# Value products over cached pages: page outermost with four requests inside, and one mark for all four

## The chip, the cores and the metric

The kernel runs on one core of a Trainium2 chip. The metric is device time in microseconds (us) of one execution; the time of the kernel before is the median of three runs. TensorE (PE) multiplies, VectorE (DVE), ScalarE (ACT) and GpSimd (POOL) do the rest, and SyncE (SP) issues most of the loads. The engines run on their own and meet at semaphores.

## The reference, cut to what matters

The program is one step of a two-layer decoder. Each layer serves one prompt of 1024 tokens and 8 sample requests of 4 tokens. Its mixer has three head groups (forgetting attention "FoX", RWKV-7, retention), then an output projection and a gated feed-forward. The change lies in FoX attention of the sample requests. Each request has 8 cached pages of 128 keys and of 128 values, with 8 heads of 64, found through a page table:

```python
def fox_sample(q, k, v, logf, k_past, v_past, logf_past):
    ...
    s_past = jnp.einsum('bthd,bshd->bhts', q, k_past, preferred_element_type=F32) * scale
    s_past = s_past + (cn[..., :, None] - cp[..., None, :])
    ...
    p = jax.nn.softmax(jnp.concatenate([s_past, s_new], -1), axis=-1).astype(v.dtype)
    return (jnp.einsum('bhts,bshd->bthd', p[..., :P], v_past)
            + jnp.einsum('bhts,bshd->bthd', p[..., P:], v))
```

The change concerns the product of the weights `p[..., :P]` with the cached values `v_past`. All is float32.

## The kernel before

Everything is written per engine, with the order by hand: a block for SP, POOL, PE, DVE and ACT, each a list of instructions with waits on semaphores. No scheduler moves anything. `Steps` numbers the marks that an engine sets in one pass of a loop (`G_PE`: PE's marks in a pass over one group of requests), so that others can wait for "mark V2 of pass it". A mark rides on the last matmul of a step.

The 8 requests are served in two groups of four: in each layer a loop `g` runs twice, `it = 2*l + g`, four passes in all. One group puts its four requests side by side in 128 partitions: request b owns partitions 32b to 32b+31 (`NS` is 32: 4 tokens by 8 heads). In one pass PE does:

- `bias`: the forget terms go to PSUM banks 0 to 2.
- For each request b, the key pages are transposed (`key_tr`, marks `T{b}{p}`, line 764 of the helper `tr`), ACT or DVE copies them out, and the scores are added to PSUM (`S{b}{p}`, helper `mm`, line 760). `p` counts pairs of heads.
- DVE and ACT do the softmax over all four requests. PE transposes the weights (`P0`, `P1`, `Pn`) into `pts`, which lies in the tile that the profile calls `hT`.
- The value products, which this change touches: first one product with the new tokens' values (`pnt` by `vn`), which opens all 128 partitions of PSUM bank 7. Then, for request b, wait for its pages, and for its eight pages j multiply `pts[:, j, 32b:32b+32]` (128 keys by 32 columns) by `slot[b][:, j, :]` (128 keys by 512) into partitions 32b to 32b+31 of bank 7. The last one carries mark `V{b}`. In the profile these are the rows `ps<-big,hT 128*32 128x512`: `slot` lies in the tile `big`. One call of `mm` in float32 gives two MATMUL instructions, each with its own weight load (engine PEld).
- DVE masks bank 7 into `om` (line 1885), PE gathers the heads (`F`, `ps<-wd 128*128 128x16`), and DVE writes the output (line 1888).

`slot[b]` holds eight pages of request b: first keys, then, when these are transposed (`T{b}3`), its values. SP loads keys (line 512) and the first five value pages (line 519), POOL the other three (line 737). On SP's queue a pass is: for b in 0 to 3, wait for `V{b}` of the pass before (line 508, the slot is free), eight key loads; then, for b in 0 to 3, wait for `T{b}3`, five value loads. Each load is preceded by a read of the page number. After the second pass of a layer SP waits for `F` and loads the weights `w_out`.

`norm_sum` (line 772) is used below as a comparison. It sends three products `ps<-sil,ones 128*32 128x352` to partitions 0, 32 and 64 of one PSUM bank, one after another.

Of the kernel before, what the change touches and what calls it, by code (L numbers as in the profile page):

```python
# [24 lines left out]
NPG, PG = 8, 128  # L25
# [13 lines left out]
NS = DB * TS  # L39
# [75 lines left out]
def build(nc, I, O, decay_rows):  # L115

    ctx = ExitStack()
    with ctx:
# [229 lines left out]
        fgr_dve, fgr_act, fgr_pe = (sem(f"foxgroup_{x}") for x in ("dve", "act", "pe"))  # L348
# [25 lines left out]
        def job_psum_tm(j):  # L374
# [66 lines left out]
                      "sn", "mx", "mn", "max", "neg", "sum", "rec", "pn", "pne", "pt1", "pnt", "om", "o")  # L441
        G_ACT = Steps(*[f"kt{b}{p}" for b in range(4) for p in (0, 2)], "e", "en", "pt0")
        G_PE = Steps("bias", *[x for b in range(4) for x in [f"T{b}0"] + [y for p in range(4) for y in ([f"T{b}{p + 1}"] if p < 3 else []) + [f"S{b}{p}"]]],
                     "P0", "P1", "Pn", "V0", "V1", "V2", "V3", "F", first=5)

        block = ctx.enter_context(nc.Block())
        w_in = I["w_in"]
# [3 lines left out]
        def _(sp):  # L451
# [31 lines left out]
            with sp.Fori(0, DEPTH) as l:  # L483
                for j in range(RING, 8):
                    free(l, j)
                    load(l, j, w_block(l, w_in, RFC[j]))
                for j0, c0_, n in ((J_EQ, C_EQ, 4), (J_EV, C_EV, 4), (J_FQ, C_FQ, 8), (J_FV, C_FV, 4)):
                    for j in range(j0, j0 + n):
                        free(l, j)
                        load(l, j, w_block(l, w_in, c0_ + P * (j - j0)))  # L490

                sp.wait_ge(table_in, 16)
                sp.wait_ge(fg_dve, FG_DVE.at(l, "vn"))
                sp.wait_ge(fp_pool, FP_POOL.at(l * 4 + 3, "k"))
                sp.wait_ge(fox_out, l * 16 + 16)
                sp.wait_ge(fox_out2, l * 16 + 16)
                sp.sem_inc(passed, 1)
                with sp.Fori(0, 2) as g:
                    it = l * 2 + g
                    for b in range(4):  # L500
                        if b == 3:

                            sp.wait_ge(fp_act, FP_ACT.at(l * 2 + 1, "1oT"))
                            sp.wait_ge(lft_out, l * 32 + 32)
                            sp.wait_ge(ko_out, l * 128 + 128)
                            sp.sem_inc(passed, 1)

                        sp.wait_ge(fgr_pe, G_PE.at(it - 1, f"V{b}"))
                        sp.sem_inc(passed, 1)
                        for j in range(NPG):  # L510
                            page = sp.value_load(ptab[0:1, bass.ds(g * (4 * NPG) + (b * NPG + j), 1)], min_val=0, max_val=N_POOL - 1)
                            sp.dma_start(slot[b][:, j, :], I["cache_fox_k"][bass.ds(l, 1), bass.ds(page, 1)].rearrange("a n p h d -> p (a n h d)")).then_inc(page_in[b], 16)

                    for b in range(4):
                        sp.wait_ge(fgr_pe, G_PE.at(it, f"T{b}3"))
                        sp.sem_inc(passed, 1)
                        for j in range(V_SP):
                            page = sp.value_load(ptab[0:1, bass.ds(g * (4 * NPG) + (b * NPG + j), 1)], min_val=0, max_val=N_POOL - 1)
                            sp.dma_start(slot[b][:, j, :], I["cache_fox_v"][bass.ds(l, 1), bass.ds(page, 1)].rearrange("a n p h d -> p (a n h d)")).then_inc(page_in[b], 16)
                    sp.sem_inc(passed, 1)  # L520

                sp.wait_ge(fgr_pe, G_PE.at(l * 2 + 1, "F"))
                for j in range(J_OUT, J_OUT + RING):
                    sp.sem_inc(passed, 1)
                    free(l, j)
                    load(l, j, w_block(l, I["w_out"], P * (j - J_OUT)))
                for j in range(J_OUT + RING, J_FF):
                    free(l, j)
                    load(l, j, w_block(l, I["w_out"], P * (j - J_OUT)))

                with sp.Fori(0, FT // 2) as q:
                    for u in range(RING):
                        sp.wait_ge(gemm_done, l * PJOBS + q * RING + (J_FF + u - RING + 1))
                        load(l, u, w_block(l, I["w_gate" if u % 2 == 0 else "w_up"], q * (2 * P) + P * (u // 2)))

                for j in range(2):
                    if j == 0:
                        sp.wait_ge(gemm_done, l * PJOBS + J_OUT + 1)
                    sp.dma_start(wd[:, j, :, :], w_block(l, I["w_down"], P * j)).then_inc(down_loaded[j], 16)
                for j in range(2, KT):  # L540
                    sp.wait_ge(gemm_done, l * PJOBS + J_DOWN + j - 2 + 1)
                    sp.dma_start(wd[:, j % 2, :, :], w_block(l, I["w_down"], P * j)).then_inc(down_loaded[j % 2], 16)

                for j in range(RING):
                    sp.wait_ge(gemm_done, l * PJOBS + JOBS - RING + j + 1)
                    sp.sem_inc(passed, 1)
                    load(0, j, w_block(DEPTH - 1 - l, w_in, RFC[j]))
# [210 lines left out]
        def _(pe):  # L758
# [53 lines left out]
            with pe.Fori(0, NTT // 2) as t:  # L812
                for u in range(2):
                    pe.wait_ge(x_in[u], t * 16 + 16)
                    pe.wait_ge(xt_ev, t * 2 + u + 1)
                    for k in range(KT):
                        last = tr(ps[:, 4 * u + k // 4, P * (k % 4):P * (k % 4) + P], xstage[:, u, P * k:P * k + P])
# [3 lines left out]
            for k in range(KT):  # L821
                last = tr(ps[:, 0, NS * k:NS * k + NS], xstage[0:NS, 0, P * k:P * k + P])
# [4 lines left out]
            with pe.Fori(0, DEPTH) as l:  # L827
# [7 lines left out]
                for m in range(2):  # L835
                    for s, (name, r0) in enumerate((("w", 0), ("a", 32))):
# [9 lines left out]
                        for b, (a, e) in enumerate(((0, 512), (512, 1024), (1024, XW))):  # L846
                            last = mm(ps[:, 4 * s + b, 0:e - a], lora[r0:r0 + 32, P * m:P * m + P], xs[r0:r0 + 32, 6, a:e])
                        PR_PE.mark(last, pr_pe, f"{name}{m}")
                for m in range(2):
                    pe.wait_ge(pr_dve, PR_DVE.at(l, f"ksq{m}"))  # L850
                    pe.wait_ge(pr_act, PR_ACT.at(l, "a1"))
                    for b, (a, e) in enumerate(((0, 512), (512, 1024), (1024, XW))):
                        last = mm(ps[:, 4 * m + b, 0:e - a], blk[:, :], sq1[m][:, a:e])
# [32 lines left out]
                with pe.Fori(0, NTT) as c:  # L886
                    it = l * NTT + c
# [58 lines left out]
                    last = mm(ps[:, 7, 0:RW], sg[64:P, :], lora[64:P, :])  # L946
# [6 lines left out]
                    for h in range(RH):  # L953
                        last = tr(ps[:, 0, P * h:P * h + P], sl[8][:, h, :])
# [13 lines left out]
                    last = x_values(3)  # L968
# [7 lines left out]
                    for h in range(RH):  # L976
                        last = mm(ps[:, 2, HD * h:HD * h + HD], sl[8][:, pos(h), :], x0(h))
# [5 lines left out]
                    for h in range(RH):  # L983
                        last = mm(y_out_(h), sl[2][:, pos(h), :], uu(h), False, True)
                    RW_PE.mark(last, rw_pe, "Y")
                    for h in range(RH):
                        last = mm(s_out(h), btok(h), uu(h), False, True)
# [6 lines left out]
                    for m in range(2):  # L994
                        last = tr(ps[:, 6, P * m:P * m + P], sl[6][:, m, :])
# [4 lines left out]
                for m in range(2):  # L1000
                    last = tr(ps[0:HD, 0, P * m:P * m + P], st[:, m, :])
# [10 lines left out]
                for m in range(2):  # L1012
                    for b in range(DB):
                        last = tr(ps[:, m, HD * b:HD * b + HD], nat[0:HD, b, P * m:P * m + P])
# [3 lines left out]
                for h in range(RH):  # L1018
# [4 lines left out]
                    last = mm(ps[SR, 4 + h % 2, NS * m:NS * m + NS], ars[r, m, 0, :], bts[r, m, :])  # L1023
                RS_PE.mark(last, rs_pe, "L")
                for m in range(2):
# [3 lines left out]
                    last = mm(ps[SR, 7, 256 + 2 * m:258 + 2 * m], rk2s[:, m, :], col2("rk", 2 * m))  # L1029
# [3 lines left out]
                for h in range(RH):  # L1033
                    last = mm(ps[SR, 0, NS * h:NS * h + NS], smat[1][SR, h, :], smat[0][SR, h, :])
# [3 lines left out]
                for h in range(RH):  # L1038
                    last = mm(ps[SR, 1, NS * h:NS * h + NS], smat[2][SR, h, :], smat[3][SR, h, :])
                RS_PE.mark(last, rs_pe, "Z2")  # L1040
                last = mm(ps[SR, 7, 0:RW], sgs[64:P, :], lora[64:P, :])
# [3 lines left out]
                for h in range(RH):  # L1045
                    m, r = h // 2, half(h)
                    o = ps[SR, 2 + h % 2, HD * m:HD * m + HD]
                    for b in range(DB):
                        mm(o, aex[r, m, b, :], sts[r, m, b, :], b == 0, False)
                    last = mm(o, smat[5][SR, pos(h), :], vts(h), False, True)  # L1050
# [3 lines left out]
                for h in range(RH):  # L1054
                    last = mm(ps[SR, 6, HD * h:HD * h + HD], smat[3][SR, pos(h), :], hd(x0s, h))
# [3 lines left out]
                for h in range(RH):  # L1059
                    m, r = h // 2, half(h)  # L1060
                    o = ps[SR, 4 - h % 2, HD * m:HD * m + HD]
# [3 lines left out]
                    last = mm(o, smat[4][SR, pos(h), :], hd(us, h), False, True)  # L1065
                RS_PE.mark(last, rs_pe, "Y")
                pe.wait_ge(*dv("vex3"))
                for h in range(RH):
                    m, r = h // 2, half(h)
                    o = ps[r, m, :]  # L1070
                    mm(o, vbks[SR, 2 + m, half(h)], uex[SR, h].rearrange("p b d -> p (b d)"), True, False)
                    last = mm(o, vbks[SR, 4 + m, half(h)], vex[SR, h].rearrange("p b d -> p (b d)"), False, True)
# [3 lines left out]
                for m in range(2):  # L1076
                    last = tr(ps[:, 6, NS * m:NS * m + NS], yns[SR, P * m:P * m + P])
# [40 lines left out]
                with pe.Fori(0, NTT) as c:  # L1118
                    it = l * NTT + c
# [136 lines left out]
                with pe.Fori(0, 2) as g:  # L1256
# [45 lines left out]
                    for b in range(4):  # L1302
                        pe.wait_ge(page_in[b], it * ((NPG + V_SP) * 16) + (NPG + V_SP) * 16)
                        pe.wait_ge(vpage_in[b], it * ((NPG - V_SP) * 16) + (NPG - V_SP) * 16)
                        o = slice(NS * b, NS * b + NS)
                        for j in range(NPG):
                            last = mm(ps[o, 7, :], pts[:, j, o], slot[b][:, j, :], False, j == NPG - 1)
                        G_PE.mark(last, fgr_pe, f"V{b}")

                    pe.wait_ge(*gd("om"))  # L1310
                    for p in range(4):
# [49 lines left out]
        def _(v):  # L1361
            def on(*waits):
                for s, val in waits:
                    v.wait_ge(s, val)
# [55 lines left out]
            with v.Fori(0, DEPTH) as l:  # L1420
# [423 lines left out]
                with v.Fori(0, 2) as g:  # L1844
# [36 lines left out]
                    gm(v.tensor_copy(pts[:, 4:8, :], ps[:, 4, :].rearrange("p (j r) -> p j r", j=4)), "pt1")  # L1881
                    on(gp("Pn"))
                    gm(v.tensor_copy(pnt[SR], ps[SR, 5, 0:P]), "pnt")
                    on(gp("V3"))
                    gm(v.tensor_tensor(om.rearrange("p (h d) -> p h d", h=FH), ps[:, 7, :].rearrange("p (h d) -> p h d", h=FH),
                                       shead.unsqueeze(2).to_broadcast((P, FH, HD)), ALU.mult), "om")
                    on(gp("F"))
# [389 lines left out]
```

## Time and profile before

| | us |
|---|---|
| median of 3 runs | 5240.82 |
| lowest and highest | 5238.62, 5245.79 |
| span of the profiled execution, first to last instruction | 5223.1 |
| PE busy in the span | 4683.3 (90%) |
| chain that ended last, PE's share | 82% |
| value products, four bursts together | 99.1 |

The profile has no total of its own for the profiled execution, only its span; the median is 17.7 us above the span. Reading: a timeline row gives the start, the time from the first start to the last end, the engine, line and operation, `out<-in` by tiles, the stationary shape (128*32 is 128 rows by 32 columns) and the moving one, and the count; in brackets the idle time of that engine just before, and what ended it. The matmuls' ends are modelled, their starts are recorded. PEclk is the granted TensorE clock: 1.00 is 2.4 GHz, 0.50 is 1.2 GHz.

### The profile page before, as it was taken

Reading aid. Unit: us, or ns where it says so; the run is one execution under the profiler, and the core shown is the slowest. Engines: PE = TensorE matmul, PEld = TensorE weight load, DVE = VectorE, ACT = ScalarE, POOL = GpSimd, SP = SyncE. Lnnn points to the kernel's source line nnn. Section 1 sums busy time; section 2 is a strip of 40 time slices with the busy share of each in tenths; the row PEclk is TensorE's granted clock in tenths of the full one; section 3 lists DMA queues with packets and bytes.
Section 4 is the critical chain, followed back from the end, with each engine's and each line's share of the span. In section 5 each row is a group of like instructions: output and inputs, shape, how many; then the busy total and the mean of one; then the engine's idle time right before and its main releaser. Section 6 shows DMA issues by size and latency. Waiting matters only on the chain.

```text
span 5223.1 us, 55407 instructions
## 1 busy us (share of the span) xinstructions
PE 4683.3 (90%) x20862; PEld 3164.5 (61%) x20862; DVE 1092.1 (21%) x2491; ACT 654.3 (13%) x1105; POOL 260.1 (5%) x456
## 2 busy tenths in 40 slices
PE   7688888988889999999995879898888999999998
PEld 4477576755445666666654766666653456666665
DVE  2344222133212000000024541312332110000001
ACT  0222011133100000000003220102231000000000
POOL 1000002100000000000010000130000000000000
PEclk8888787989899999999997888798998999999999
DMA  3300101102241111111112001011024211112011
GB/s 75 17 0 0 38 21 23 42 26 65 93 139 33 36 40 36 36 41 34 39 38 5 0 5 41 13 35 42 13 65 157 86 33 36 36 36 58 22 34 61
DMA packets 274079, 215.20 MB, mean 41 GB/s; under 512 B 23696, under 2 KB 236912, under 8 KB 272640
## 3 DMA queue, kind: packets, MB, share of 16 engines
q1 hardware_dynamic: 255296, 163.64, 12.2%
q0 software_dynamic: 18624, 49.50, 3.4%
q8 instruction: 93, 1.52, 0.1%
q14 instruction: 66, 0.54, 0.1%
HBM read 197.55 MB, written 15.53 MB: 41 GB/s over the span
## 4 chain that ended last, share of the span: by engine, by line
PE 82%; DVE 7%; issue 5%; ACT 3%; DMA 3%; DVEq 0%; POOL 0%; ACTq 0%; POOLq 0%; SPq 0%
PE ps L760 79%; PE ps L764 3%; DMA out_rwkv_shift_sample<-big 1%; DVE hT L1379 1%; ACT wd L2136 1%; DMA big<-in_x_prompt 0%; DVE big L1571 0%; DMA wd<-in_state_rwkv 0%; ACT wd L2123 0%; ACT big L2106 0%; DMA out_y_prompt<-big 0%; ACT sil L2152 0%; DVE sil L1372 0%; DVE big L1579 0%; DVE big L1541 0%
## 5 line engine op out<-in xcount | busy, mean ns | idle before, releaser
L760 PE MATMUL ps<-hT,ring 128*128 128x352 f32 x6528 | 1966.1, 463 | 25.6 <-DVE hT L1379 10.7
L760 PEld LDWEIGHTS ps<-hT,ring 128*128 128x128 f32 x6528 | 1246.7, 192 | 738.7 <-issue 29.1
L760 PE MATMUL ps<-big,wd 128*128 128x352 f32 (+3 forms) x2576 | 711.6, 439 | 65.5 <-ACT big L1969 42.3
L760 PEld LDWEIGHTS ps<-big,wd 128*128 128x128 f32 (+2 forms) x2576 | 462.5, 192 | 311.5 <-ACT big L1969 42.6
L1901 DVE TENSOR_TENSOR big<-ps,sil 128x1056 f32 x44 | 55.3, 1258 | 1189.5 <-PE ps L760 1189.5
L760 PE MATMUL ps<-wd 128*128 128x128 f32 (+4 forms) x1560 | 235.0, 297 | 70.0 <-ACT wd L2136 21.7
L760 PE MATMUL ps<-big 128*128 128x128 f32 (+4 forms) x1488 | 244.0, 337 | 52.5 <-POOL big L636 14.8
L760 PEld LDWEIGHTS ps<-wd 128*128 128x128 f32 (+2 forms) x1560 | 207.1, 203 | 136.5 <-issue 76.2
L760 PE MATMUL ps<-ring,hT 128*128 128x128 f32 (+1 forms) x2304 | 261.5, 275 | 0.0
L764 PE MATMUL ps<-ident,big 128*128 128x128 f32 (+4 forms) x998 | 175.4, 322 | 95.4 <-ACT big L1992 28.3
L760 PEld LDWEIGHTS ps<-ring,hT 128*128 128x128 f32 (+1 forms) x2304 | 256.9, 183 | 5.2 <-issue 2.4
L760 PEld LDWEIGHTS ps<-big 128*128 128x128 f32 (+2 forms) x1488 | 203.5, 222 | 86.1 <-issue 16.7
L764 PEld LDWEIGHTS ps<-ident,big 128*128 128x128 f32 (+4 forms) x998 | 131.3, 162 | 123.3 <-issue 67.5
L2164 ACT ACTIVATE sil<-ps 128x1056 f32<-128x1056 f32 x44 | 46.3, 1051 | 1162.8 <-PE ps L760 1162.8
L760 PE MATMUL ps<-sil,wd 128*128 128x64 f32 (+2 forms) x544 | 175.4, 438 | 3.6 <-ACT sil L2152 3.6
L1906 DVE TENSOR_TENSOR xT<-ps,xT 128x1056 f32<-128x1056 f32 x16 | 20.1, 1257 | 599.9 <-PE ps L760 599.9
L2123 ACT ACTIVATE wd<-wd,big 128x256 f32<-128x256 f32 (+7 forms) x128 | 99.2, 775 | 301.7 <-DVE big L1805 301.7
L764 PE MATMUL ps<-ident,wd 128*128 128x128 f32 (+1 forms) x644 | 104.2, 298 | 35.7 <-DVE wd L1877 18.1
L760 PE MATMUL ps<-big,sil 64*128 64x64 f32 (+4 forms) x560 | 116.9, 391 | 8.3 <-DVE sil L1710 8.3
L760 PE MATMUL ps<-ring,wd 128*128 128x128 f32 (+1 forms) x584 | 90.2, 300 | 36.5 <-ACT wd L2136 25.7
L760 PE MATMUL ps<-big,ring 128*128 128x352 f32 x384 | 121.4, 459 | 0.0
L760 PE MATMUL ps<-sil 64*128 64x256 f32 (+4 forms) x608 | 81.8, 420 | 40.6 <-DVE sil L1489 37.7
(336 smaller groups left out, 3122.6 us busy)
## 6 DMA issues: line engine op xcount, KB each, us to landing
big<-in_cache_fox_k SPq DMA_DIRECT2D x128, 256.0 KB, 2.9
ring<-in_w_in SPq DMA_DIRECT2D x60, 512.0 KB, 3.8
ring<-in_w_gate SPq DMA_DIRECT2D x44, 512.0 KB, 3.8
ring<-in_w_up SPq DMA_DIRECT2D x44, 512.0 KB, 3.8
wd<-in_w_down SPq DMA_DIRECT2D x16, 1408.0 KB, 7.0
big<-in_cache_fox_v SPq DMA_DIRECT2D x80, 256.0 KB, 4.0
big<-in_cache_fox_v POOLq DMA_DIRECT2D x48, 256.0 KB, 4.3
ring<-in_w_out SPq DMA_DIRECT2D x16, 512.0 KB, 4.1
```

Of the source, the lines that this page charges most:

```text
L760: return pe.matmul(out, lhsT, rhs, start=start, stop=stop, skip_group_check=True)
L764: return pe.transpose(out, in_, ident[0:n, 0:n])
L1379: NRM_DVE.mark(v.scalar_tensor_tensor(hT[:, k, :].rearrange("p (a b) -> p a b", a=3), xT[:, k, :].rearrange("p (a b) -> p a b", a=3), col( ...
L1901: v.tensor_tensor(big[:, bass.ds((q * 2 + u) * NT, NT)].rearrange("p (a b) -> p a b", a=3), job_psum(1), sil[:, u * NT:(u + 1) * NT].rearr ...
L1906: v.tensor_tensor(xk, job_psum(j), xk, ALU.add).then_inc(evac[j % 2], 1)
L2123: fm(act(sp_[:, s % 2, 0:w], sp_[:, s % 2, 0:w], ACT.Exp, bias=nmx[:, s:s + 1], accum_out=rsum[:, s:s + 1]), f"{u}e{s}")
L2136: fm(a.copy(ptt[:, 0, 0:s // 2 + 1, :], ps[:, 4:6, :].rearrange("p a (b c) -> p (a b) c", c=P)[:, 0:s // 2 + 1, :]), f"{u}pt{s}")
L2164: act(sil[:, u * NT:(u + 1) * NT].rearrange("p (a b) -> p a b", a=3), job_psum(0), ACT.Silu).then_inc(evac[0], 1)
```

## The change

The loop over requests first waits for the pages of all four. Then the loop over pages is outside and the loop over requests inside. Four marks `V0` to `V3` become one mark `V`; SP waits for it before the key loads of every request, and DVE before `om`. The number and the shapes of the products are as before.

```diff
                     for b in range(4):
                         pe.wait_ge(page_in[b], it * ((NPG + V_SP) * 16) + (NPG + V_SP) * 16)
                         pe.wait_ge(vpage_in[b], it * ((NPG - V_SP) * 16) + (NPG - V_SP) * 16)
-                        o = slice(NS * b, NS * b + NS)
-                        for j in range(NPG):
+                    for j in range(NPG):
+                        for b in range(4):
+                            o = slice(NS * b, NS * b + NS)
                             last = mm(ps[o, 7, :], pts[:, j, o], slot[b][:, j, :], False, j == NPG - 1)
-                        G_PE.mark(last, fgr_pe, f"V{b}")
+                    G_PE.mark(last, fgr_pe, "V")
...
-                        sp.wait_ge(fgr_pe, G_PE.at(it - 1, f"V{b}"))
+                        sp.wait_ge(fgr_pe, G_PE.at(it - 1, "V"))
...
-                    on(gp("V3"))
+                    on(gp("V"))
```

On PE, at the value products of a pass. `ps` is PSUM, `pages_in{b}` and `last_v_pages_in{b}` are the semaphores of the loads by SP and by POOL. Before:

```order
L760 MATMUL ps<-ring,wd 128x512 [waits foxgroup_act]
L1303 REGISTER_ALU
L1304 ISA [waits pages_in0]
L760 MATMUL ps<-big,hT 32x512 [waits last_v_pages_in0]
L760 MATMUL ps<-big,hT 32x512 x7
L760 MATMUL ps<-big,hT 32x512 [waits last_v_pages_in1,pages_in1]
L760 MATMUL ps<-big,hT 32x512 x7
L760 MATMUL ps<-big,hT 32x512 [waits last_v_pages_in2,pages_in2]
L760 MATMUL ps<-big,hT 32x512 x7
L760 MATMUL ps<-big,hT 32x512 [waits last_v_pages_in3,pages_in3]
L760 MATMUL ps<-big,hT 32x512 x7
```

The same place now:

```order
L760 MATMUL ps<-ring,wd 128x512 [waits foxgroup_act]
L1303 REGISTER_ALU
L1304 ISA [waits pages_in0]
L760 MATMUL ps<-big,hT 32x512 [waits last_v_pages_in2,pages_in2,pages_in3,last_v_pages_in1,last_v_pages_in3,pages_in1,last_v_pages_in0]
L760 MATMUL ps<-big,hT 32x512 x31
```

The waits for requests 1 to 3 have moved ahead of the first product, and the 32 products stand in one row with no wait between them; which request each belongs to, these rows don't show (the diff does).

On SP, where the key loads of request 1 begin (`ptab` is the page table, `foxgroup_pe` the semaphore of PE's marks); difference of the two:

```order
 L512 DMA big<-in_cache_fox_k 128x512
-L508 REGISTER_ALU
 L511 ISA [waits foxgroup_pe]
 L511 TENSOR_LOAD ptab
```

The wait stays ahead of each request's loads; the register that held the number of `V{b}` is no longer stepped, since all four wait for the same mark.

## Rows read from the trace of the kernel before

**Rows 1.** Page, part 4: shares of the chain that ended last.
```profile
PE 82%; DVE 7%; issue 5%; ACT 3%; DMA 3%; DVEq 0%; POOL 0%; ACTq 0%; POOLq 0%; SPq 0%
```
**Rows 2.** Groups by line and shape, whole span: busy us, mean ns, idle before.
```profile
L760 PE MATMUL ps<-big,hT 128*32 128x512 f32 x256 | 99.1, 631 | 0.0
```
**Rows 3.** Timeline, layer 1: first value burst, and the second pass's keys.
```profile
1417.90 25.01 PE L760 MATMUL ps<-big,hT 128*32 128x512 f32 x64
1428.38 40.81 SPq L512 DMA_DIRECT2D big<-in_cache_fox_k  x32
...
1449.58 3.67 PE L764 MATMUL ps<-ident,big 128*128 128x128 f32 x16
...
1474.49 1.97 PE L764 MATMUL ps<-ident,big 128*128 128x128 f32 x16
```
**Rows 4.** Timeline, layer 1: second value burst to the output projection.
```profile
1470.17 30.10 SPq L519 DMA_DIRECT2D big<-in_cache_fox_v  x20
...
1507.52 24.58 PE L760 MATMUL ps<-big,hT 128*32 128x512 f32 x64
...
1538.54 4.47 PE L760 MATMUL ps<-hT,ring 128*128 128x352 f32 x8 [4.59 <-DMA ring<-in_w_out]
...
1547.57 2.53 PE L760 MATMUL ps<-big,ring 128*128 128x352 f32 x8
1549.94 2.53 PE L760 MATMUL ps<-hT,ring 128*128 128x352 f32 x8
```
**Rows 5.** Timeline of PE, layer 2: both value bursts.
```profile
3991.64 24.97 PE L760 MATMUL ps<-big,hT 128*32 128x512 f32 x64
...
4081.22 24.55 PE L760 MATMUL ps<-big,hT 128*32 128x512 f32 x64
```
**Rows 6.** Timeline of PEld: weight loads early in the first burst, then request 0 to 1.
```profile
1418.76 0.18 PEld L760 LDWEIGHTS ps<-big,hT 128*32 128x32 f32 x1 [0.68 <-issue]
1419.61 0.18 PEld L760 LDWEIGHTS ps<-big,hT 128*32 128x32 f32 x1 [0.68 <-issue]
...
1425.07 0.11 PEld L760 LDWEIGHTS ps<-big,hT 128*32 128x32 f32 x1 [0.32 <-issue]
1425.49 0.14 PEld L760 LDWEIGHTS ps<-big,hT 128*32 128x32 f32 x3 [0.32 <-issue]
1425.92 0.14 PEld L760 LDWEIGHTS ps<-big,hT 128*32 128x32 f32 x2 [0.29 <-issue]
1426.35 0.14 PEld L760 LDWEIGHTS ps<-big,hT 128*32 128x32 f32 x2 [0.29 <-issue]
```
**Rows 7.** Timeline, one norm_sum: six products to three column groups, and what follows.
```profile
1568.96 0.15 PEld L760 LDWEIGHTS ps<-sil,ones 128*32 128x32 f32 x6 [0.49 <-issue]
1568.97 0.79 PE L760 MATMUL ps<-sil,ones 128*32 128x352 f32 x6
...
1569.69 0.86 PE L760 MATMUL ps<-hT,ring 128*128 128x352 f32 x2
```
**Rows 8.** Windows, layer 1: PE, PEld, DVE, ACT, POOL busy, PEclk, DMA share, GB/s.
```profile
1412.56:1422.80 10.24, 9.07 (x17) 3.26 (x18) 1.35 (x4) 1.87 (x2) 0.00 (x0) 0.50 0.13 49
...
1446.69:1453.52 6.83, 6.83 (x23) 4.77 (x22) 0.23 (x1) 1.01 (x1) 0.00 (x0) 0.50 0.74 212
1501.31:1511.55 10.24, 8.21 (x16) 3.09 (x17) 2.14 (x6) 0.59 (x1) 0.00 (x0) 0.50 0.16 59
...
1535.44:1542.27 6.83, 3.73 (x7) 2.22 (x8) 0.00 (x0) 0.00 (x0) 0.00 (x0) 0.50 0.99 282
```
**Rows 9.** Request 0's key loads, second pass (timeline), and landings, 1425 to 1445.
```profile
1428.38 9.56 SPq L512 DMA_DIRECT2D big<-in_cache_fox_k  x8
...
big<-in_cache_fox_k SPq DMA_DIRECT2D x13, 256.0 KB, 2.9
```
**Rows 10.** Request 3's value loads, first pass (timeline), and landings, 1455 to 1505.
```profile
1405.60 5.05 SPq L519 DMA_DIRECT2D big<-in_cache_fox_v  x5
...
big<-in_cache_fox_v SPq DMA_DIRECT2D x20, 256.0 KB, 3.9
```

More of the change, by code:

```diff
@@ L443, in build @@
         G_PE = Steps("bias", *[x for b in range(4) for x in [f"T{b}0"] + [y for p in range(4) for y in ([f"T{b}{p + 1}"] if p < 3 else []) + [f"S{b}{p}"]]],
-                     "P0", "P1", "Pn", "V0", "V1", "V2", "V3", "F", first=5)
+                     "P0", "P1", "Pn", "V", "F", first=5)
         block = ctx.enter_context(nc.Block())
```

## Prediction

> **What bounds the kernel now.** The chain that ended last comes first: PE holds 82% of it [rows 1], so time taken from PE on that chain counts in full until something else is late. Next the groups by shape: the value products are 256 MATMUL instructions, 99.1 us of PE [rows 2]. That is the whole stage the change touches, and no other engine works for PE in it. The timeline shows it as four bursts of 64 instructions, one per pass, of 25.0, 24.6, 25.0 and 24.6 us [rows 3 to 5]. Nobody has work beside a burst except SP, which loads the next pass's keys during the first burst of a layer [rows 3].
>
> The question is how densely the 64 stand. The weight loads tell. Within a request one follows the other at 0.85 us at the low clock and 0.43 us at the high one [rows 6]; all 16 instructions of a request go to the same 32 columns of the array. At the passage from request 0 to 1 the picture differs: three loads within 0.14 us, then twice two [rows 6]. The tail of request 0 and the head of request 1 run side by side, since they use different columns. Without that, a first burst would be 4.9 us at the low clock (1417.9 to 1422.8, [rows 3, 8]; 5.8 instructions of 0.85) and 58.2 of 0.43, 30.0 us with 0.2 for the last one's end. It takes 25.0, so each of the three passages saves 1.7 us, four instructions. The overlap across columns exists already, but only at three points of a burst.
>
> **The change part by part.**
>
> *The order of the products.* With pages outside, two instructions of request 0 are followed by two each of requests 1, 2 and 3, in four different column groups. Whether they then run four abreast is the main term. Norm_sum has this form for three groups: six weight loads start within 0.15 us, and the next stage's first matmul starts 0.72 us after the first of the six [rows 7]. One after the other, at the spacing of the same 352-column form (eight in 2.37 us, 0.30 each, [rows 4]), they would need 1.78; two steps abreast need 0.60 and one end. So three groups, three different moving operands and one PSUM bank don't brake each other. At a passage between requests, request 1 starts while three of request 0's instructions still stand in front [rows 6]; to start request 3 abreast in a page, one each of requests 0, 1 and 2 must be passed, also three. I take four abreast: 16 steps for 64 instructions.
>
> A burst then takes: first pass, 4.9 us at the low clock (5.8 steps), 10.2 steps of 0.43, 0.2 for the end: 9.5 us. Second pass: low from 1507.5 to 1511.55 [rows 4, 8], 4.7 steps, then 11.3 of 0.43: 9.1 us. I let the clock rise as long after the burst's start as now, because what precedes the burst on PE is unchanged. The ends: at the high clock throughout 7.1 us, at the low one throughout 13.8. I take the middle, where the rows lie. Saved: 15.5 us per burst, of which not all is kept.
>
> The Trainium skill, "TensorE: Matmul & The Clock Gate", Part 3 (Packing small matmuls), gives 2.38-fold for three column groups of 32 with 512 moving columns. The share of the ideal carried over to four groups would be 3.17-fold, an estimate: 11.2 us for a first burst in place of 9.5, and about 5201 us in all. The trace's norm_sum gives 1.78 over 0.72, 2.5-fold, but a train of 16 steps pays its end once and one of two steps pays it at a half; so the rows' sum stands.
>
> *The mark and SP's key loads.* Now SP may load request 0's next keys once V0 is done. The last load of V0 stands at 1426.35, its matmul one step later, with some 0.6 us to run [rows 2, 6]: done at 1427.4, and the first key load is issued 1.0 us later, at 1428.38. Eight issues take 9.56 us, the last starts at about 1437.6 and lands 2.9 us later, at 1440.5 [rows 9]. PE takes those keys at 1449.58 [rows 3], so 9.1 us of slack hide them. With the change the mark comes at the end of the burst, 1417.9 + 9.5 = 1427.4, by chance when V0 came. The keys are thus there at 1440.5 as now, 13.1 us after the burst's end, but PE is ready 6.7 us after it (1442.9 to 1449.58 now). This becomes a new wait of 6.4 us in the first pass of each layer: PE's key transposes start at 1440.5, not at 1434.1. The gain there is 15.5 - 6.4 = 9.1 us.
>
> Queued behind SP's wait are the 32 key loads and the 20 value loads of the second pass. Their spacing is SP's own: 40.81 us for 32 [rows 3], 10.2 per request. PE took 24.9 us from request 0's keys to request 2's (1449.58 to 1474.49, [rows 3]), the first of the two the slower, since it began at the low clock [rows 8]. SP needs 20.4 for two, so request 2's keys would be there at 1460.9 and asked for at 1465.4, and request 1's lie between with some 2 us of cover. No second wait.
>
> *The joint wait for values.* In the first pass the last of request 3's SP loads is issued by 1410.7 and landed by about 1414.2 [rows 10], before the burst at 1417.9. So the joint wait ends before the burst; it costs nothing, 3.7 us of cover. In the second pass PE comes 9.1 us earlier while SP's key loads don't, so the cover shrinks: value loads begin at 1470.17 as now [rows 4], four sets at some 6.0 us (5.05 and the next set's wait and first page number), the last issued at 1493.2 and landed at 1497.1. The burst would start at about 1498.4. Cover 1.3 us; I price the wait at 0, at most 2 us.
>
> *The end of a layer.* After the second burst nothing is prefetched that the burst hides: `w_out` is issued after F in both orders, and its 4.6 us wait [rows 4] stays. The second burst's 15.5 us are kept.
>
> *The clock after it.* PE now idles before the key transposes, and the work that lifts the clock is cut in two. Now the clock is back 3.9 us after 1449.58 and 3.7 us after 1538.54 [rows 3, 4, 8]; the longest stretch at the low level here, 1412.56 to 1422.80, is 10.2 us [rows 8]. If it comes back later by 0 to 6 us, half of that is lost: 0 to 3 us after each burst. Nearest are the two values at 3.7 to 3.9, so I take small losses, 1.0 us at the keys, 0.5 at `w_out`.
>
> Sum per layer: 9.1 - 1.0 + 15.5 - 0.5 = 23.1; two layers 46.2. The trace's span would go from 5223.1 to 5176.9, and with the 17.7 us between span and median the median from 5240.8 to 5194.6 us.
>
> **The rivals.**
>
> *Fewer abreast.* If only three groups run at once, a burst has 21.3 steps, 11.8 and 11.4 us; gains 6.8 and 13.2, less 1.5, 18.5 per layer: 5203.8 us. If two, 32 steps, 16.4 and 16.0 us: 2.2 + 8.6 - 1.5 = 9.3 per layer, 5222.2. For it speaks that no row shows four groups at once; against it that three run without a brake and that neighbours overlap at all three passages, by the sum of 30.0 against 25.0 us above.
>
> *No overlap, slower.* If each request's pair must be done before the next request's may start, the page order takes away the three overlaps that exist and adds the key wait: a burst of 30.0 us (29.6), 5.0 more each, and 6.4 of key wait in the first pass, with 1.5 of clock: 17.9 per layer, 35.8 in all, 5276.6 us. The sign turns where bursts last 20.9 us (25.0 + 24.6 less 6.4 and 1.5, halved), 42 steps: fewer than 1.5 products abreast in the mean. The six loads in 0.15 us speak against it. The same page of the Trainium skill, Part 3, says that a weight load overlaps with running matmuls only if the row groups differ; here all use the same 128 rows, and by that rule this rival would hold. The trace disagrees: three loads within 0.14 us over the same rows while request 0 was still running [rows 6].
>
> *The waits eat it.* The gain stays on paper if keys or values land later than worked out, for instance because value loads of POOL now meet SP's key loads sooner. Only the first pass's 9.1 us and some of the second's can go: at worst 2 x 9.1 lost, 5213 us.
>
> **How the numbers follow.** Four abreast 82%, with waits as worked out or up to that worst case; three abreast 4%; two abreast 6%; none 6%; and 2% that the two effects cancel. The forecast is 5194.6. With every burst at the high clock: 11.5 + 17.5 per layer without clock loss, 58 us, 5182.8. With every burst at the low clock and clock losses of 2.9 and 1.6: 4.8 + 10.8 - 4.5 = 11.1 per layer, 5218.6. Allowing 2 us for the spread of medians, the range is 5181 to 5221; the pairs and the no-overlap case lie outside. A measurement of this kernel tells 0.2%, some 10 us, from no change: faster 0.92, same 0.02, slower 0.06.
>
> **What would show it.** Right: bursts of 8 to 11 us with weight loads in clusters of about eight per 0.85 us; a new idle time of PE before the keys' transposes put down to a key load, 4 to 8 us, in the second pass of each layer only; the `w_out` wait as now. Wrong: loads still one per 0.43 us (no overlap), or in threes or twos (fewer abreast); PE idle before the first value product, put down to a value load; a stretch at clock 0.50 that covers whole bursts. The forecast fails most simply if the fourth column group or SP's key loads don't behave as their nearest rows do.

## The result, and the profile after

The changed kernel took 5190.91 us in the median of four runs (5186.18 to 5192.62), the kernel before 5241.09 (5238.62 to 5245.79): ratio 0.9911, 95% interval 0.9891 to 0.9932. It is faster, by 50 us against the 46 forecast, and 3.7 us from the forecast time.

The groups by shape over the whole span, to set against [rows 2]:

```profile
L760 PE MATMUL ps<-big,hT 128*32 128x512 f32 x256 | 38.0, 760 | 0.0
```

The same 256 instructions occupy PE for 38.0 us instead of 99.1. The mean of one has grown from 631 to 760 ns: no single instruction became faster (its modelled length is 1.06 us at the low clock and 0.59 at the high one in both traces); four run side by side, and a larger share of them at the low clock. The timeline of layer 1, to set against [rows 3, 4, 6]:

```profile
1424.39 0.20 PEld L760 LDWEIGHTS ps<-big,hT 128*32 128x32 f32 x8 [1.50 <-issue]
1424.39 9.43 PE L760 MATMUL ps<-big,hT 128*32 128x512 f32 x64
1425.25 0.20 PEld L760 LDWEIGHTS ps<-big,hT 128*32 128x32 f32 x4 [0.66 <-issue]
...
1429.36 0.12 PEld L760 LDWEIGHTS ps<-big,hT 128*32 128x32 f32 x4 [0.50 <-issue]
1429.79 0.12 PEld L760 LDWEIGHTS ps<-big,hT 128*32 128x32 f32 x4 [0.31 <-issue]
...
1434.88 9.56 SPq L512 DMA_DIRECT2D big<-in_cache_fox_k  x8
...
1437.11 4.00 PE L760 MATMUL ps<-wd 64*128 64x512 f32 x6 [1.39 <-DVE wd L1856]
1447.10 3.68 PE L764 MATMUL ps<-ident,big 128*128 128x128 f32 x16 [6.00 <-DMA big<-in_cache_fox_k]
...
1473.03 1.97 PE L764 MATMUL ps<-ident,big 128*128 128x128 f32 x16
...
1476.44 23.52 SPq L519 DMA_DIRECT2D big<-in_cache_fox_v  x20
...
1506.06 9.56 PE L760 MATMUL ps<-big,hT 128*32 128x512 f32 x64
1522.18 5.06 PE L760 MATMUL ps<-hT,ring 128*128 128x352 f32 x8 [4.67 <-DMA ring<-in_w_out]
...
1534.71 2.53 PE L760 MATMUL ps<-hT,ring 128*128 128x352 f32 x8
```

The first row holds the loads of two steps. After it four weight loads lie within 0.12 us at the high clock (0.20 at the low one), and the next four follow one step later: 0.85 us at the low clock, 0.43 at the high one. A burst is 16 steps. The row of key loads has request 0's eight alone, to set against the 9.56 us of [rows 9]. Behind the first burst stands the new wait, 6.00 us, put down to a key load. No burst has a wait for value pages ahead of it, and the wait for `w_out` is 4.67 us (4.6 before). Layer 2:

```profile
3977.57 9.43 PE L760 MATMUL ps<-big,hT 128*32 128x512 f32 x64
...
4000.17 3.68 PE L764 MATMUL ps<-ident,big 128*128 128x128 f32 x16 [5.90 <-DMA big<-in_cache_fox_k]
4059.18 9.58 PE L760 MATMUL ps<-big,hT 128*32 128x512 f32 x64
```

The windows, to set against [rows 8]; the figure behind the five busy times is the granted clock:

```profile
1418.96:1429.20 10.24, 8.98 (x35) 3.38 (x39) 1.44 (x4) 1.87 (x2) 0.00 (x0) 0.50 0.15 58
...
1436.02:1453.09 17.07, 9.99 (x25) 5.65 (x26) 2.04 (x6) 1.01 (x1) 0.00 (x0) 0.50 0.72 201
1500.88:1511.12 10.24, 9.23 (x35) 3.38 (x39) 1.19 (x4) 0.58 (x1) 0.00 (x0) 0.50 0.16 61
1517.94:1528.18 10.24, 6.00 (x10) 3.53 (x11) 0.00 (x0) 0.00 (x0) 0.00 (x0) 0.50 0.77 205
```

The clock is low for 4.8 us of the first burst and 5.1 of the second, then for 6.0 us from the start of the key transposes (3.9 before) and 6.0 from the start of `w_out` (3.7 before).

**Where the time went.** From the first burst's start to the second's, layer 1 took 89.6 us [rows 3, 4] and takes 81.7: 7.9 saved. From the second burst's start to the fifth group of `w_out`, the row at 1549.94 in [rows 4] and at 1534.71 after, it took 42.4 and takes 28.7: 13.8 saved. That is 21.7 us, and layer 2 saves as much.

For all kernels below, one stretch is measured from the starts in the trace: from the last score product of a layer's first pass to the hundredth 128x352 product of `w_out`, both layers added. "Rest" is the span less the stretch.

| kernel | stretch, us | rest, us |
|---|---|---|
| before, first profile | 325.1 | 4898.0 |
| before, second profile (e0) | 322.8 | 4906.1 |
| changed | 281.6 | 4906.3 |
| changed again (e7) | 281.5 | 4909.9 |
| e1, old order, one wait, one mark | 336.6 | 4896.4 |
| e2, pairs | 296.4 | 4906.0 |
| e3, own marks | 278.5 | 4895.1 |
| e4, page numbers ahead | 274.5 | 4906.2 |
| e5, fill | 262.2 | 4907.6 |
| e6, fill and page numbers | 253.7 | 4917.1 |
| e8, more fill | 253.9 | 4899.7 |
| e9, as e6 | 258.8 | 4919.9 |
| e10, as e5 | 265.5 | 4907.4 |

The change is worth 42 us in the stretch (324.0 less 281.5). The rest holds the same instructions in every kernel here, but that SP reads request 0's page numbers earlier in e4, e6, e8 and e9; it spreads over 25 us between profiles. The medians' 50 us, 40 when the changed kernel was run again (e7), and the 35 between the two profiles' spans are those 42 with this spread.

### The profile page after: what moved, and what is told of

It is laid out like the page before. It is cut to its first block, busy times and chain, and to the rows that moved or that the text cites. A ratio compares the mean times of both kernels' runs of the same rounds, so it can differ in the third digit from the quotient of the medians.

```text
span 5187.9 us, 55395 instructions
## 1 busy us (share of the span) xinstructions
PE 4638.1 (89%) x20862; PEld 3157.1 (61%) x20862; DVE 1092.3 (21%) x2491; ACT 654.0 (13%) x1105; POOL 260.2 (5%) x456
## 4 chain that ended last, share of the span: by engine, by line
PE 81%; DVE 7%; issue 5%; ACT 3%; DMA 3%; DVEq 0%; SPq 0%; POOL 0%; ACTq 0%; POOLq 0%
PE ps L760 78%; PE ps L764 4%; DMA out_rwkv_shift_sample<-big 1%; DVE hT L1380 1%; ACT wd L2137 1%; DMA big<-in_x_prompt 0%; DVE big L1572 0%; DMA wd<-in_state_rwkv 0%; ACT big L2107 0%; ACT wd L2124 0%; ACT sil L2153 0%; DVE sil L1373 0%; DMA out_y_prompt<-big 0%; DVE big L1580 0%; DVE big L1542 0%
## 5 line engine op out<-in xcount | busy, mean ns | idle before, releaser
L760 PE MATMUL ps<-hT,ring 128*128 128x352 f32 x6528 | 1968.2, 463 | 24.7 <-DVE hT L1380 10.0
L760 PE MATMUL ps<-wd 128*128 128x128 f32 (+4 forms) x1560 | 238.5, 300 | 70.1 <-ACT wd L2137 21.7
L2165 ACT ACTIVATE sil<-ps 128x1056 f32<-128x1056 f32 x44 | 46.2, 1050 | 1164.0 <-PE ps L760 1164.0
```

The costliest lines, as they stand in the source:

```text
L760: return pe.matmul(out, lhsT, rhs, start=start, stop=stop, skip_group_check=True)
L2165: act(sil[:, u * NT:(u + 1) * NT].rearrange("p (a b) -> p a b", a=3), job_psum(0), ACT.Silu).then_inc(evac[0], 1)
```

## The experiments

**e1: the old order, with the new wait and mark.**

```diff
-                    for j in range(NPG):
-                        for b in range(4):
+                    for b in range(4):
+                        for j in range(NPG):
```

> The changed kernel with the products in the order of before (all eight pages of request 0, then of request 1, and so on), but with its one joint wait and its one mark. Theory (the order gives the gain, the one mark only delays the next keys): bursts of 24.6 to 25.0 us as before, and PE waits some 6.4 us more for the second pass's keys than before, since SP's mark comes at the burst's end; with 0.5 to 1 us of low clock per layer that is 13 to 16 us over before: 5254 to 5257 us. Rival (fewer waits and marks between the products are what makes them fast): bursts near 9.5 us and about 5191 us.

Measured: 5247.04 us against 5230.94 for the kernel before on the same chip, ratio 1.0029 (1.0018 to 1.0040), 16 us slower by the medians; in the stretch 12.6 us more. Its timeline of PE, first burst and keys, then weight loads at the passage from request 0 to 1:

```profile
1418.09 24.95 PE L760 MATMUL ps<-big,hT 128*32 128x512 f32 x64
...
1456.23 3.67 PE L764 MATMUL ps<-ident,big 128*128 128x128 f32 x16 [6.41 <-DMA big<-in_cache_fox_k]
```

```profile
1425.18 0.11 PEld L760 LDWEIGHTS ps<-big,hT 128*32 128x32 f32 x1 [0.32 <-issue]
1425.61 0.14 PEld L760 LDWEIGHTS ps<-big,hT 128*32 128x32 f32 x3 [0.32 <-issue]
1426.04 0.14 PEld L760 LDWEIGHTS ps<-big,hT 128*32 128x32 f32 x2 [0.29 <-issue]
1426.47 0.14 PEld L760 LDWEIGHTS ps<-big,hT 128*32 128x32 f32 x2 [0.29 <-issue]
1426.93 0.11 PEld L760 LDWEIGHTS ps<-big,hT 128*32 128x32 f32 x1 [0.32 <-issue]
```

The bursts are as long as before, the key wait is there. The single wait and mark by themselves cost; the gain comes with the order. With no wait between the requests the overlap at a passage is still the same few instructions, so it is not the waits that kept it short in the kernel before.

**e2: two requests abreast.**

```diff
-                    for j in range(NPG):
-                        for b in range(4):
+                    for half in range(2):
+                        for j in range(NPG):
+                            for b in (2 * half, 2 * half + 1):
```

> The changed kernel, but page by page with only requests 0 and 1 inside, then page by page with requests 2 and 3. Theory (time goes with the number of column groups abreast): 32 steps instead of 16, bursts of 15 to 16.4 us, 5.5 to 6.9 us more per burst than with four: 5213 to 5219 us. Rival (two groups already fill what PE or its memory ports can take, the fourfold order adds nothing): bursts of about 9.5 us and 5191 us. Rival (each further group slows the others): bursts under 14 us.

Measured: 5204.97 us, ratio 0.9943 (0.9921 to 0.9965); stretch 296.4, between the two. The median lies 8 us below the 5213 to 5219 expected. Its first burst and weight loads:

```profile
1418.29 14.56 PE L760 MATMUL ps<-big,hT 128*32 128x512 f32 x64
```

```profile
1424.92 0.11 PEld L760 LDWEIGHTS ps<-big,hT 128*32 128x32 f32 x2 [0.32 <-issue]
1425.35 0.11 PEld L760 LDWEIGHTS ps<-big,hT 128*32 128x32 f32 x2 [0.32 <-issue]
1425.77 0.15 PEld L760 LDWEIGHTS ps<-big,hT 128*32 128x32 f32 x6 [0.32 <-issue]
1426.20 0.15 PEld L760 LDWEIGHTS ps<-big,hT 128*32 128x32 f32 x4 [0.28 <-issue]
```

Two per step (more where the second pair begins beside the end of the first), each step as long as with four. So time goes with the number of steps, and neither two groups nor four slow each other. The bursts (14.3 to 14.6 us) are 0.4 to 0.7 under the bounds I gave and 1.8 under the rival's 16.4: the tail of the first pair runs beside the head of the second, four steps of 0.43, a term I had left out there.

**e3: only the loops changed, own waits and marks kept.**

```diff
-                    for b in range(4):
-                        pe.wait_ge(page_in[b], ...)
-                        pe.wait_ge(vpage_in[b], ...)
-                        for j in range(NPG):
+                    for j in range(NPG):
+                        for b in range(4):
+                            if j == 0:
+                                pe.wait_ge(page_in[b], ...)
+                                pe.wait_ge(vpage_in[b], ...)
...
+                            if j == NPG - 1:
+                                G_PE.mark(last, fgr_pe, f"V{b}")
```

> The kernel before with only the order of the loops changed: pages outside, requests inside; each request keeps its own wait (ahead of its first product) and its own mark V0 to V3 (on its last product). Theory: as the changed kernel within 2 us, 5189 to 5193 us, bursts of 9.4 to 9.6 us, keys awaited for 6 us, since all four marks fall on the last page anyway. Rival (the joint wait or the single mark has a price or a gain of its own): more than 4 us away from the changed kernel.

Measured: 5186.84 us, 44 under the kernel before on the same chip (ratio 0.9920, 0.9898 to 0.9942); the changed kernel was 50 and 40 under its own. The stretch is 278.5 against 281.5: its bursts are 8.6 and 9.4 us long because the clock came back 3.1 and 3.2 us after the start of the first bursts, not 4.8. The key wait is there as well (7.09 us in layer 1). The median lies 2 us below the range I had given, and 4 and 6 us under the two medians of the changed kernel, past the 4 us that I had set for the rival; but those come from other chips or series, and the ratios to the kernel before (0.9920 here, 0.9911 and 0.9924) agree within their intervals. The marks and waits have no price of their own that these runs can tell.

**e0: the kernel before, second profile.**

> The kernel before once more, for a second profile. The first profile's span (5223.1) lies 15 us under what the median run would have. If that is spread in stages which the change doesn't touch (the clock's return in the RWKV and retention parts), this profile has a span nearer 5238, its value bursts are again 24.5 to 25.0 us, and the difference lies ahead of the first burst and between the layers' bursts.

Measured: one run, 5230.47 us; span 5228.9, so not 5238 as expected; bursts 24.1 to 24.7 us; stretch 322.8, within 2.3 us of the first. The rest is 8 us longer than in the first profile. The stages ahead of the first burst already spread: it starts at 1417.90 in the first profile and 1422.85 in this one. Another 3.6 us lie between the two layers' stretches, as expected.

**e7: the changed kernel again, base of the next three.**

> The changed kernel itself, as the base for the three that follow on the same chip: 5186 to 5193 us, bursts of 9.4 to 9.6 us, key wait 6.0 us in the second pass of each layer.

Measured: 5192.55 us, 40 under the kernel before (5232.94) on the same chip, ratio 0.9924 (0.9907 to 0.9940); stretch 281.5, bursts 9.35 to 9.57.

**e4: the new key wait, cut at SP.**

```diff
+                        pages = [sp.value_load(ptab[...]) for j in range(NPG)] if b == 0 else None
                         sp.wait_ge(fgr_pe, G_PE.at(it - 1, "V"))
...
-                            page = sp.value_load(ptab[...])
+                            page = pages[j] if pages else sp.value_load(ptab[...])
```

> The changed kernel, but SP reads the eight page numbers of request 0 before it waits for mark V, so that after the mark only the eight key loads themselves are issued. Theory (the new key wait is SP's issue time, 1.28 us per load of which some 0.8 is the read of the page number): eight issues in 3.5 to 4.5 us instead of 9.6, keys there 5 to 6 us earlier, the wait falls from 6.0 to 0 to 2 us, 8 to 13 us less in all than the changed kernel. Rival (the transfers themselves are the limit, 256 KB each): the wait falls by less than 2 us, under 4 us in all.

Measured: 5174.40 us, ratio 0.9882 (0.9865 to 0.9898); the stretch falls by 7.0, the median by 18 with the rest's spread in it. SP's issues after the mark, then PE's keys:

```profile
1430.27 4.77 SPq L513 DMA_DIRECT2D big<-in_cache_fox_k  x8
```

```profile
1439.61 3.68 PE L765 MATMUL ps<-ident,big 128*128 128x128 f32 x16 [2.44 <-DMA big<-in_cache_fox_k]
```

And the DMA share (last but one figure) while they land:

```profile
1434.00:1436.00 2.00, 2.00 (x4) 0.78 (x3) 0.00 (x0) 0.00 (x0) 0.00 (x0) 0.50 0.99 294
1436.00:1438.00 2.00, 1.17 (x4) 0.56 (x2) 0.00 (x0) 0.00 (x0) 0.00 (x0) 0.50 0.90 330
```

Eight issues take 4.77 us instead of 9.56, and the wait falls from 6.00 to 2.44. SP's issue time was the main part of it, 3.6 of 6.0 us. Reading a page number thus took some 0.6 us per load (9.56 less 4.77, over eight), where I had taken 0.8. The gain is 3.5 us per layer, not the 5 to 6 expected. The last of the eight is issued by 1435.04 and PE starts 4.6 us later, where the median load took 2.9 us in [rows 9], and the DMA engines are 0.9 to 1.0 busy meanwhile. So the transfers are the likely limit of what is left; no run here shortens them to show it.

**e5 and e10: the clock ahead of the burst.**

```diff
+                    for _ in range(18):
+                        mm(ps[:, 6, 0:P], ident[:, :], ident[:, :])
                     pe.wait_ge(*gd("pn"))
```

> The changed kernel with 18 products of the identity by itself added on PE, into a bank nobody reads, in the gap in which PE waits for the softmax (4.5 us idle before the burst). They compute nothing that is used. Theory (about 2.4 us of each burst, and more of the transposes ahead of it, are lost to the low clock that the gap brings): the clock stays at 1.00, bursts of 7.1 us, 3 to 5 us less per pass, 12 to 20 us less in all than the changed kernel. Rival (the gap isn't what brings the clock down, or such products don't hold it): bursts stay at 9.4 to 9.6 us, 0 to 4 us more in all.

> The kernel of e5 once more (18 products in the softmax gap), beside e9 on the same chip: 5165 to 5178 us; bursts of 7.1 us wherever the clock stays at 1.00 ahead of them.

Measured: 5165.81 us (ratio 0.9868, 0.9852 to 0.9885) and, in the second series, 5176.12 (0.9893, 0.9874 to 0.9911). Stretches 262.2 and 265.5, 16 to 19 us under the changed kernel; the medians lie 27 and 16 us under e7, with the rest's spread in them. Two windows of e5: from the second pass's last score product to its burst, with the fill, and that burst.

```profile
1493.03:1501.06 8.03, 6.78 (x51) 5.42 (x49) 3.81 (x11) 2.07 (x5) 0.54 (x2) 1.00 0.75 272
1501.06:1508.10 7.04, 7.04 (x65) 1.97 (x64) 0.00 (x0) 0.00 (x0) 0.00 (x0) 1.00 0.00 0
```

Where PE is occupied in the gap and the clock stays at 1.00, the burst takes the 7.1 us worked out for it. The fill does not always hold the clock: in one of e5's four passes and two of e10's it was low at about the start of the burst all the same, and these bursts took 8.49, 8.46 and 8.77 us; over the five profiles with the fill (e5, e6, e8, e9, e10) it was so in 8 of 20. Why in these, the runs don't show. So up to 2.4 us of a burst, and what the low clock costs ahead of it, come from the softmax gap.

**e6 and e9: both together.** The two edits above in one kernel.

> Both of the above: page numbers of request 0 read ahead, and the 18 products in the softmax gap. Theory (two separate terms of one chain): the two gains add up, 20 to 33 us less than the changed kernel, 5158 to 5171 us. Rival (a shorter burst only lengthens the key wait): clearly less than the sum.

> The kernel of e6 once more, with more rounds. In its first profile the touched stretch was 253.7 us against 281.5 of the changed kernel, so the two gains added up there (7.0 and 19.3 alone), but the median was not below that of the fill alone. If the stages that the change doesn't touch spread by some 10 us from run to run, the median is now 20 to 32 us below the changed kernel (5160 to 5172 us) and not above that of the fill alone. Rival (reading ahead costs something elsewhere): again above the fill alone by 5 us or more, with the excess in one place of the trace.

Measured: 5172.43 us (0.9883, 0.9866 to 0.9899) and 5167.30 (0.9878, 0.9862 to 0.9895). In the stretch the gains add up in the first profile: 27.8 under the changed kernel, 7.0 and 19.3 alone; in the second 22.7, where three of four bursts met a fallen clock (8.4 to 8.6 us). Its median was first above and then below that of the fill alone. The rest of its two profiles is the longest of all (4917.1, 4919.9). Most of the excess lies between the two layers' stretches, 2419 and 2425 us from the end of one to the start of the other against 2412 and 2416 in the changed kernel. Of the edits only the earlier reading of page numbers reaches into that part. It is not shown to cost there: e2 and e10 are without it and take 2419 and 2418, and e8 has it and takes 2410, the least of all. The granted clock goes along with it. Summed over that part, PE had the low clock for 396 us in e6 and 403 in e9, against 382 and 386 in the changed kernel and 376 in e8; over the 13 profiles the part is longer by some 0.4 us for each microsecond more at the low clock. Why a profile has more or less of it stays open.

**e8: the fill in the smaller gaps too, on top of e6.**

```diff
                     G_PE.mark(last, fgr_pe, "V")
+                    for _ in range(3):
+                        mm(ps[:, 6, 0:P], ident[:, :], ident[:, :])
...
                     G_PE.mark(last, fgr_pe, "F")
+                    for _ in range(5):
+                        mm(ps[:, 6, 0:P], ident[:, :], ident[:, :])
+                for _ in range(15):
+                    mm(ps[:, 6, 0:P], ident[:, :], ident[:, :])
```

> Page numbers read ahead and 18 products in the softmax gap, as in e6, and the same fill in the smaller gaps: 3 behind the burst, 5 behind F, 15 more in the wait for w_out at a layer's end. They compute nothing that is used. Theory (idle PE brings the low clock, which then slows the key transposes and the start of w_out): the clock stays at 1.00 from the burst to the keys and into w_out, 2 to 3 us less at each of the two places, 8 to 12 us less than e6 in the stretch from the last score of the first pass to w_out, both layers together. Rival (the fill delays what it covers, or the clock falls all the same): within 3 us of e6.

Measured: 5153.54 us, ratio 0.9851 (0.9835 to 0.9868), the fastest kernel here; but its stretch is 253.9, as in e6. The expected 8 to 12 us aren't in it. The timeline of PE:

```profile
1426.56 2.10 PE L761 MATMUL ps<-wd 64*128 64x512 f32 x6 [0.18 <-DVE wd L1865]
1432.82 3.67 PE L765 MATMUL ps<-ident,big 128*128 128x128 f32 x16 [4.16 <-DMA big<-in_cache_fox_k]
...
1504.77 2.63 PE L761 MATMUL ps<-hT,ring 128*128 128x352 f32 x8
```

`w_out` now starts at the full clock (2.63 us for the first group, 5.06 in the changed kernel). The bias products are faster too, 2.10 us instead of 4.00, but the keys don't come earlier, so the wait grows from 2.4 to 4.2 us, the clock falls in it, and it comes back 5.5 us after the transposes' start, where it came back 2.9 us after it in e6. What e8 gained at `w_out` it lost there and in second bursts of 8.4 to 8.6 us, at whose start the clock was low. Its median is 14 us under e9's, and all its four runs (5150.81 to 5155.20) lie under all of e9's. Of the 25 us between the two profiled executions 20 are the rest (4899.7 and 4919.9); whether the rest makes up the medians' 14 as well, or the fill has an effect there, one profile of e8 can't tell.

## Why the prediction was right, point by point

- **Four abreast.** Right, and it was the main term. Loads come in fours, e2 shows that a step is as long with four as with two, and e1 that without the order nothing is gained. A burst measures 9.43, 9.56, 9.43 and 9.58 us, against 9.5 and 9.1. The second was 0.5 too low because the clock returned 5.1 us after its start, not 4.0. Each such burst is 7.07 us (e5) and half of its time at the low clock: 7.07 + 5.1 / 2 = 9.6.
- **No overlap.** The rival fell. The Trainium skill ("TensorE: Matmul & The Clock Gate", Part 3) says that weight loads overlap running matmuls only if the row groups differ. Here four loads over the same 128 rows lie within 0.12 us and the burst shortens to 9.4 us; the measurement decides against the rule as it stands there, for different column groups. The estimate from that page's 2.38-fold, 11.2 us per burst, was too high as well.
- **The key wait.** Right: PE took the keys 13.3 us after the burst's end (1424.39 + 9.43 to 1447.10) against 13.1, and waited 6.00 and 5.90 us against 6.4. e4 shows that 3.6 us of it are SP's reading of the page numbers ahead of its issues.
- **No further wait.** Right. The 20 value loads of the second pass are issued in 23.5 us, 23.0 forecast; the last is issued by 1499.96 and with the 3.9 us of [rows 10] landed by 1503.9, ahead of the burst at 1506.06. By this estimate the cover was 2.2 us, 1.3 forecast. `w_out`'s wait stayed.
- **The clock afterwards.** At the keys 1.0 us as taken: from request 0's transposes to request 2's 25.9 us after, 24.9 before. At `w_out` 1.1 us (12.5 from its first group to its fifth, 11.4 before), where I had taken 0.5.
- **The sum.** 21.7 per layer in the traces against 23.1: 8 as forecast in the first pass, 13.8 against 15.0 in the second, from the burst and `w_out`. The forecast time came out 3.7 us off, closer than its terms were known: the sum was 46.2 us, the stretch shows 42, the medians differ by 50 and 40. That the rest's spread fell on the right side is luck.
- **Span and median.** One step was wrong in kind without harm. I took the 17.7 us between the profile's span and the median for something that lies around the span. In the run of the changed kernel with a profile, 5189.39 us stand beside a span of 5187.9: only 1.5 us lie around it. The first profile of before was one from the fast end of the rest's spread. The 2 us that I allowed for the spread of medians were too few as well: four medians of the kernel before lie between 5230.47 and 5241.09 us.

## What to carry to other kernels

Products that use only 32 of the array's columns cost as much as full ones when they stand one behind the other: 0.43 us for 512 moving columns, where the full 128*128 form took 0.30 for 352 [rows 4], at the high clock, the same per column. They cost about a quarter of that when four of them with different output partitions alternate, here each with its own weights and moving operand. Array columns and output partitions go together in every kernel here, so these runs can't say which of the two must differ. Look at whether the weight loads come singly or in clusters. The score products of this kernel have the same form, 256 with 124.1 us in the changed kernel, and their rows still show four of one request in 1.90 us at the high clock, one behind the other; whether they could alternate no run here tries. What was hidden under the longer burst (here the next keys) comes to light, and its price, 6 of 15 us, can be read beforehand from when the mark will come and how long the loads behind it take. Judge such a change by its own stretch of the trace when the rest of the program spreads by half as much as the gain.

## What the runs showed that was not expected

- The stages outside the stretch add up to 4895 to 4920 us from profile to profile. The granted clock goes along with it: between the layers by the sums given with e6 and e9, and ahead of the first burst in the window from 268 to 288 us, in the RWKV stage. The clock there was 0.97 in the first profile of before and 0.74 in that of the changed kernel, whose first burst starts 6.5 us later. In the six profiles with 0.93 or more the last score product of the first pass starts at 1405.7 to 1408.6 us, in the six with 0.74 or less at 1413.1 to 1418.1. What sets the clock there, these runs don't settle.
- Eighteen products of no use in a 4.5 us gap were worth 16 to 19 us over four passes, nearly half as much as the change itself.
- Issuing eight key loads in 4.8 us instead of 9.6 brought the keys only 3.5 us earlier, with the DMA engines at 0.9 to 1.0.
